# Renumbering the attention units so that the two halves of TensorE's array alternate (one-core streaming encoder step, f32)

## What is computed

```
B_HEAD_DIM = 64; B_Q_HEADS = 16; B_KV_HEADS = 4; CHUNK = 64; META = 16; WINDOW = 128
s_meta = jnp.einsum('bnqkgd,bjkd->bkgnqj', q, k_meta) * scale
s_loc = jnp.einsum('bnqkgd,bnjkd->bkgnqj', q, kb) * scale
p_meta, p_loc = sink_softmax(s_meta, s_loc, mask, sinks_r)
out = (jnp.einsum('bkgnqj,bjkd->bnqkgd', p_meta, v_meta)
       + jnp.einsum('bkgnqj,bnjkd->bnqkgd', p_loc, vb))
```

## Time and profile before

| | us |
|---|---|
| median of 3 runs (2803.07 to 2807.3) | 2803.46 |
| the profiled execution | 2798.76 |
| its span | 2797.0 |
| PE busy in the span | 2654.5 (95%) |
| attention block, its first DMA issue to the next block's first load | 1620.56 to 1817.31 |
| one prompt step of the loop | 7.66 |
| mean granted clock of TensorE over the span | 0.976 |

### The profile page before, as it was taken

One profiled execution on the slowest core, in us unless ns is written; L12 is line 12 of the kernel. 1 busy time (PEld: TensorE's weight loads), 2 busy tenths in 40 slices (PEclk: granted clock), 3 DMA queues, 4 the chain that ended last, 5 costly groups with the idle time before them and its releaser, 6 DMA issues. The chain is left out here.

```text
span 2797.0 us, 37740 instructions
## 1 busy us (share of the span) xinstructions
PE 2654.5 (95%) x15390; PEld 2593.3 (93%) x15390; DVE 1088.3 (39%) x2197; ACT 636.5 (23%) x1390; POOL 603.1 (22%) x503
## 2 busy tenths in 40 slices
PE   8999999989999999999978957898999999999998
PEld 7988898989999999999978946798999999999997
DVE  6444455153233333332374326524433333233334
ACT  5222223041111111111123314312211111111112
POOL 2212213211221222112233430022122212121211
PEclk9999999999999999999999969999999999999999
DMA  4544454111111111111113254331111111111111
GB/s 141 150 128 136 137 171 135 54 30 46 46 32 45 46 46 38 46 38 46 31 55 90 74 115 100 73 114 38 38 46 46 38 46 38 46 45 40 43 41 76
DMA packets 272768, 191.79 MB, mean 69 GB/s; under 512 B 53144, under 2 KB 259756, under 8 KB 272580
## 3 DMA queue, kind: packets, MB, share of 16 engines
q1 hardware_dynamic: 246324, 174.27, 21.4%
q10 hardware_dynamic: 25520, 15.04, 2.0%
q0 software_dynamic: 768, 0.27, 0.0%
HBM read 148.74 MB, written 42.34 MB: 68 GB/s over the span
## 5 line engine op out<-in xcount | busy, mean ns | idle before, releaser
L584 POOL TENSOR_TENSOR wl<-raw,wh 128x512 fp32r<-128x512 f32 x260 | 331.8, 1301 | 1329.5 <-ACT wh L576 1329.5
L706 PE MATMUL psum<-xh,wl 128*128 128x400 f32 (+1 forms) x1872 | 430.0, 338 | 0.0
L706 PE MATMUL psum<-xl,wh 128*128 128x400 f32 (+1 forms) x1872 | 428.3, 337 | 0.0
L706 PE MATMUL psum<-xh,wh 128*128 128x400 f32 (+1 forms) x1872 | 427.2, 336 | 0.0
L848 DVE TENSOR_TENSOR h<-h,psum 128x384 f32<-128x384 f32 (+1 forms) x528 | 264.5, 552 | 285.0 <-PE psum L726 267.3
L706 PEld LDWEIGHTS psum<-xh,wl 128*128 128x128 f32 x1872 | 336.6, 188 | 0.0
L706 PEld LDWEIGHTS psum<-xl,wh 128*128 128x128 f32 x1872 | 336.5, 188 | 0.0
L706 PEld LDWEIGHTS psum<-xh,wh 128*128 128x128 f32 x1872 | 335.8, 188 | 0.0
L1498 PE MATMUL psum<-xh,wh 128*128 128x384 f32 (+1 forms) x792 | 274.7, 347 | 5.2 <-DVE xl L1640 2.4
L1498 PE MATMUL psum<-xl,wh 128*128 128x384 f32 (+1 forms) x792 | 270.5, 342 | 0.0
L1498 PE MATMUL psum<-xh,wl 128*128 128x384 f32 (+1 forms) x792 | 269.4, 340 | 0.0
(11 more groups left out here) (237 smaller groups left out, 3582.1 us busy)
## 6 DMA issues: line engine op xcount, KB each, us to landing
raw<-in_w_gate_up SPq DMA_DIRECT2D x88, 512.0 KB, 3.9
raw<-in_w_down SPq DMA_DIRECT2D x44, 512.0 KB, 3.6
raw<-in_a_w_in SPq DMA_DIRECT2D x24, 512.0 KB, 4.7
fr_qkv<-qkv_d SPq DMA_DIRECT2D x36, 256.0 KB, 4.1
qkv_d<-fr_tmp SPq DMA_DIRECT2D x32, 192.0 KB, 2.0
qr_d<-tmp ACTq DMA_DIRECT2D x8, 584.0 KB, 2.8
x_loaded<-og_d SPq DMA_DIRECT2D x8, 584.0 KB, 5.7
hn_d<-fr_hn_turned SPq DMA_DIRECT2D x36, 128.0 KB, 3.3
```

The lines of the kernel that those rows point to most:

```text
L584: pool.tensor_tensor(wl[:, p % 3, v], raw[:, self.raw_of(p), v], wh[:, p % 3, v].bitcast(F32), ALU.subtract).then_inc(self.w_lo, 1)
L706: y = pe.matmul(psum[:, bank + c, 0:nt], w[:, k, :], x[:, k, t0:t0 + nt], start=(k == 0 and m == 0), stop=(k == KD - 1 and m == 2))
```

## The change

A table `UNITS` gives unit `un` its KV head and half: (0,0), (1,0), (0,1), (1,1), (2,0), (3,0), (2,1), (3,1). PE issues score and value matmuls in the order (kh 0, half 0), (kh 0, half 1), (kh 1, half 0), and so on, so neighbours use different halves of the array and, in the scores, different PSUM banks. In the values the two window matmuls of a pair come first, then the two meta matmuls. Decode scores loop over KV head, sequence, half, and each half has its own bank. The semaphores still count after four units. What follows from the numbering: the sinks are loaded by 8 smaller DMAs instead of 4, the waits for them go from 64 to 128, the decode maxima are two instructions instead of one, and the exponentials of decode look up where their unit's scores stand. The diff, cut:

```diff
+    UNITS = [(0, 0), (1, 0), (0, 1), (1, 1), (2, 0), (3, 0), (2, 1), (3, 1)]
+    PAIRS = [(kh, hf) for kh in range(KVH) for hf in range(2)]
...
-            pool.wait_ge(cst, 64)
+            pool.wait_ge(cst, 128)
...
-                    for b in range(SB):
-                        for un in range(NU):
-                            kh, half = un % KVH, HD * (un // KVH)
-                            x = pe.matmul(psum[R * b:R * b + R, 2 * g + un // 4, (un % 4) * SK:(un % 4 + 1) * SK],
+                    for kh in range(KVH):
+                        for b in range(SB):
+                            for hf in range(2):
+                                half = HD * hf
+                                x = pe.matmul(psum[R * b:R * b + R, 2 * g + hf, kh * SK:(kh + 1) * SK],
...
-                for un in range(NU):
-                    if later(i) and un % KVH == 0:
-                        pe.wait_ge(ex, i * 2 + (un // KVH - 1) if un else i * 2 - 1)
-                    kh, half = un % KVH, HD * (un // KVH)
+                for kh, hf in PAIRS:
+                    un, half = UNITS.index((kh, hf)), HD * hf
+                    if later(i) and hf == 0 and kh % 2 == 0:
+                        pe.wait_ge(ex, i * 2 if kh else i * 2 - 1)
...
-                    if kh == KVH - 1:
+                    if kh % 2 and hf:
                         x.then_inc(sc, 1)
...
-                for un in range(NU):
-                    kh, half = un % KVH, HD * (un // KVH)
-                    if kh == 0:
-                        pe.wait_ge(pts, i * 2 + (1 + un // KVH))
+                for kh in range(KVH):
+                    if kh % 2 == 0:
+                        pe.wait_ge(pts, i * 2 + (1 + kh // 2))
+                    outs = [psum[HD * hf:HD * hf + HD, 7, kh * P:(kh + 1) * P] for hf in range(2)]
+                    units = [UNITS.index((kh, hf)) for hf in range(2)]
                     if dec:
                         for b in range(SB):
-                            x = pe.matmul(psum[half:half + HD, 7, kh * P + R * b:kh * P + R * b + R],
-                                          vct[:, (i - NP) * SB + b, kh * HD:(kh + 1) * HD],
-                                          pt[0:SK, un, R * b:R * b + R], start=True, stop=True)
+                            for hf in range(2):
+                                x = pe.matmul(outs[hf][:, R * b:R * b + R],
+                                              vct[:, (i - NP) * SB + b, kh * HD:(kh + 1) * HD],
+                                              pt[0:SK, units[hf], R * b:R * b + R], start=True, stop=True)
                     else:
-                        o = psum[half:half + HD, 7, kh * P:(kh + 1) * P]
-                        pe.matmul(o, vw[0:w, kh * HD:(kh + 1) * HD], pt[0:w, un, :], start=True, stop=False)
-                        x = pe.matmul(o, vm[:, un, :], pm[:], start=False, stop=True)
+                        for hf in range(2):
+                            pe.matmul(outs[hf], vw[0:w, kh * HD:(kh + 1) * HD], pt[0:w, units[hf], :],
+                                      start=True, stop=False)
+                        for hf in range(2):
+                            x = pe.matmul(outs[hf], vm[:, units[hf], :], pm[:], start=False, stop=True)
...
-                        u = slice(KVH * half, KVH * half + KVH)
-                        act.dma_start(sink[j * CHUNK:(j + 1) * CHUNK, u], src.to_broadcast([CHUNK, KVH]))\
-                            .then_inc(cst, 16)
+                        for g in range(2):
+                            dst = sink[j * CHUNK:(j + 1) * CHUNK, 4 * g + 2 * half:4 * g + 2 * half + 2]
+                            act.dma_start(dst, src[:, 2 * g:2 * g + 2].to_broadcast([CHUNK, 2])).then_inc(cst, 16)
```

More of the change, by code:

```diff
@@ L2003, in _ @@
                 sp.dma_start(vm[META * un:META * un + META, un, :],
-                             kv[0:META, 0, 1, (un % KVH) * HD:(un % KVH + 1) * HD]).then_inc(vml, 16)
+                             kv[0:META, 0, 1, UNITS[un][0] * HD:(UNITS[un][0] + 1) * HD]).then_inc(vml, 16)
             load(2, WINDOW, 0)
@@ L2065, in scores @@
                         pe.wait_ge(ex, 2 * i)
-                    for b in range(SB):
-                        for un in range(NU):
-                            kh, half = un % KVH, HD * (un // KVH)
-                            x = pe.matmul(psum[R * b:R * b + R, 2 * g + un // 4, (un % 4) * SK:(un % 4 + 1) * SK],
-                                          qd[half:half + HD, g * SB + b, 2 * kh:2 * kh + 2, :],
-                                          ks[half:half + HD, g * SB + b, kh, :], start=True, stop=True)
+                    for kh in range(KVH):
[3 more added lines that the diff above has]
+                                x = pe.matmul(psum[R * b:R * b + R, 2 * g + hf, kh * SK:(kh + 1) * SK],
+                                              qd[half:half + HD, g * SB + b, 2 * kh:2 * kh + 2, :],
+                                              ks[half:half + HD, g * SB + b, kh, :], start=True, stop=True)
                     x.then_inc(sc, 2)
@@ L2179, in exponentials @@
                 for un in range(NU):
-                    x = act.activation(pb[:, u, un, 0:width(i)], src[:, un // per, un % per, :], ACT.Exp,
+                    at_ = UNITS[un][0] + KVH * UNITS[un][1] if decode(i) else un
+                    x = act.activation(pb[:, u, un, 0:width(i)], src[:, at_ // per, at_ % per, :], ACT.Exp,
                                        scale=SCORE_SCALE, bias=st[:, u, 2, un:un + 1], accum_out=st[:, u, 3, un:un + 1])
@@ L2216, in _ @@
                 dve.tensor_copy(kv[0:n, g, :, :].rearrange("p x d -> p (x d)"), psum[0:n, 4 + g, :]).then_inc(kve, 1)
-            dve.wait_ge(cst, 64)
+            dve.wait_ge(cst, 128)
             def maxima(i, u):
@@ L2224, in maxima @@
                 per = 4 if decode(i) else 2
-                out = st[:, u, 0, :].rearrange("p (b u) -> p b u", u=per)
-                halves = 1 if decode(i) else 2
-                m = NU // per // halves
-                for x in range(halves):
+                out = st[:, u, 0, :].rearrange("p (b u) -> p b u", u=2)
+                for x in range(2):
                     dve.wait_ge(sc, i * 2 + (2 if decode(i) else x + 1))
-                    y = dve.tensor_reduce(out[:, x * m:(x + 1) * m], unit_scores(i, per)[:, x * m:(x + 1) * m], AX_X,
-                                          ALU.max)
+                    if decode(i):
+                        out = st[:, u, 0, :].rearrange("p (g h k) -> p h g k", g=2, h=2)[:, x]
+                        src = unit_scores(i, per)[:, x].rearrange("p (g k) s -> p g k s", g=2)
+                        y = dve.tensor_reduce(out, src, AX_X, ALU.max)
+                    else:
+                        y = dve.tensor_reduce(out[:, 2 * x:2 * x + 2], unit_scores(i, per)[:, 2 * x:2 * x + 2], AX_X,
+                                              ALU.max)
                 y.then_inc(mx, 1)
```

## The result

The changed kernel takes 2776.01 us (median of 4 runs, 2775.57 to 2778.38) against 2803.69 of the kernel before in the same comparison: 27.7 us less, ratio 0.9903 with an interval of 0.989 to 0.9915. In the excerpts of traces and code, `...` stands for lines left out.

The account below looks back on a forecast made before the run. DVE and ACT were taken to bound the prompt loop, PE being late by only 0.24 us a step. Terms 3.4 + 3.2 + 1.5 + 3.2 + 1.5 - 0.2 = 12.6 us gave 2790.9 us; range 2781 to 2801.

Parts of the forecast that it names:

- (f): Sinks' 8 DMAs at the stage's start: nothing, ends +2.8 us or as much gained; split decode maxima cost 0.2 us.
- (a): Step 0's values and step 2's maxima at half clock: values 5.7 instead of 9.8 us, 3.4 us saved.
- (b): The 13 other prompt steps: DVE's remaining waits for prompt scores go, 3.2 us.
- (c): Step 3's values at half clock and the scores, after the cached keys are turned: 1.5 us gained, ends 0 and 2.7.
- The ceiling: Prompt loop: however fast PE becomes, a step can lose 0.24 us, not more.
- the ring: Prompt loop: dependencies through DVE and ACT set the step at about 7.42 us; it was 7.66 with PE late.
- (d): Two decode steps: prompt values ahead of each give 1.1 us, decode scores 0.5; together 3.2 us.
- the seam's rate: Where the old values switch halves, two units take 0.50 instead of 0.87 us; for decode scores 0.047 us per record.
- (e): Last 64 records of decode values, 6.61 us at half clock: 1.5 us gained, ends 0 and 2.8.
- rival "more": Whole attention: all ceilings reached and full clock back earlier, 22 us gained, 2781 us; chance 15%.
- rival of a loss by the clock: Prompt loop loses the full clock: +2.0 us a step, 2818 us with all twelve steps; chance 6%.
- signs that the prediction named for being wrong: Clock drops between 1700 and 1800 us, loop step stays at 7.66 us, or stage's first transposes move over 1 us.

Follow-up runs that it names:

- experiment 1: Kernel before with only the sinks loaded by 8 DMAs of two columns instead of 4 of four: 2797.64 us against 2805.35, ratio 0.998.
- experiments 2 and 6: Changed kernel with half the sinks' DMAs behind cached loads (2780.64 us), cached loads after K/V rows (2775.19), cached loads on SP (2776.29, 2771.6), sinks as one row (2775.6), last two together (2768.3).
- Experiment 4: Changed kernel with decode scores looping over sequence, KV head, half instead of KV head, sequence, half: one execution 2779.35 us.
- half of the sinks last: Changed kernel with four of its eight sink DMAs issued behind the loads of cached keys and decode queries: 2780.64 us, ratio 0.9914.
- cached keys on SP: Changed kernel with cached keys, values and decode queries loaded on SP's queue behind step 2's loads, GpSimd's weight preparation split: 2776.29 us, ratio 0.9903.
- step 3 ahead: Changed kernel with cached loads on SP, step 3's Q, K and V loads issued ahead of them, GpSimd's first weights prepared later: 2771.6 us, ratio 0.9889.
- both: Changed kernel with cached loads on SP behind step 3's loads, and sinks loaded as one row to each partition: 2768.27 us, ratio 0.9877.

## Why the prediction was wrong

**(f) failed, and is the largest error: 0 forecast, 6.35 us measured at the first maxima.** The step read: "so I take nothing", as the cached keys are needed late and DVE comes late to its wait for the sinks. Both are true and beside the point: the question was what else is in the queues. What experiment 1 shows in its place is that the eight DMAs alone bring the first maxima 6.4 us forward and the time to 0.998 of the old one, some 6 us less. That they do it because ACT's later cached loads let SP's K and V rows go first is read from the queues; experiments 2 and 6 give the position of the cached loads and the pieces of the sinks a part each.

**(a) came to its number partly by luck, and was eaten: 3.4 forecast, 3.66 measured, then 2.62 us lost** in step 2 to 3, where the earlier statistics of DVE met GpSimd's split. I had asked what comes late on PE's path, not what a neighbour does at the new time. The 3.4 us were what a wait for K ahead of step 2's scores would leave, and that wait did not come (the one of 3.78 us came in step 1, where it cost nothing: maxima 0 to 1 are 5.69 us apart before and 5.70 after). PE's rows from step 0's values to its next transposes:

```profile
1650.65 0.69 PE L2121 MATMUL psum<-at_prob_turned,at_v_window 64*64 64x128 f32 x4 [1.92 <-DMA at_v_meta<-at_kv_rows]
1651.27 0.69 PE L2124 MATMUL psum<-at_prob_meta_turned,at_v_meta 128*64 128x128 f32 x4
...
1655.63 0.69 PE L2061 MATMUL psum<-ident,at_v 128*128 128x128 f32 x2
```

A group of two takes 0.62 us, what one matmul took before (0.61), not 0.71; the values take 4.98 instead of 9.83 us. What held the gain down was another transfer, the meta rows of V: the values start 4.95 us after the second maxima instead of 2.82.

**(b) and (c): 4.7 forecast, 5.0 measured.** The ceiling held as a mechanism, but the ring was 7.33 and not 7.42 us: when PE is early, the maxima follow the V copy after 0.33 instead of 0.42 us. A pair costs 0.44 us, not the 0.50 of the one seam in the old order, whose neighbours on either side still ran alone.

**(d): 3.0 forecast, 5.5 measured.** The failed step was "I take 0.5, being next to the seam's rate". That the old order overlaps here already was right, but the seam's rate (0.047 us per record, scaled from another form) is that of two tiles at work and no floor. Experiment 4 shows 1.95 us with two tiles in strict turn and 1.00 with eight, 0.016 us per record (1.00 / 64); even the end of half of 3.29 us was passed.

**(e): 1.5 forecast, 4.9 measured.** The failed step was to take the middle between nothing and 2.8 us: the values overlap fully, at either clock (6.61 to 3.63, 3.68 to 2.06), so the order alone gives 3.0. The other part is the clock, which stayed up in the profiled execution. The rival "more" named both, with 2.8 us for this term and 15% for the case, and was still 5 us short, since a gain by (f) was in no case.

The rival of a loss by the clock, at 6%, came in a small dose. The stretch of 1700 to 1740 us, before and after:

```profile
1700.00:1740.00 40.00, 34.73 (x311) 30.80 (x309) 26.79 (x65) 19.13 (x91) 0.00 (x0) 1.00 0.53 115
```

```profile
1700.00:1740.00 40.00, 26.91 (x312) 22.58 (x313) 29.27 (x73) 19.66 (x99) 0.00 (x0) 0.94 0.60 130
1726.00:1728.00 2.00, 2.00 (x20) 1.62 (x16) 1.05 (x4) 0.91 (x6) 0.00 (x0) 0.50 0.00 0
```

With PE less busy the clock is at its lower level for parts of the loop. The changed kernel's loop steps are 7.32 to 7.35 us but for one of 7.42, so it paid 0.1 us; in four of the other kernels with the new order (half of the sinks last, cached keys on SP, step 3 ahead, both) one step of the loop took 8.35 us. Of the signs that the prediction named for being wrong, two were there: this drop of the clock, and the first transposes of the stage, which moved from 23.21 to 16.85 us after its start.

With three of the changed kernel's terms off by 6.4, 2.5 and 3.4 us in the same direction, a range of 10 us on either side could not hold the time. It was built from the bounds of the terms, and the one bound that was passed over was that of (f), whose working named a gain of 2.8 us as an end; in the range it stood on the slow side only.

What stays open: 5 of the 27.7 us stand between the medians and the profiles, since the profiled execution of the kernel before was 4.7 us faster than its median. The last values don't explain it, since that execution had them at the lower clock already. The first decode values can be slow too (5.74 instead of 3.68 us in the profile of experiment 1), which would be 2 of the 4.7. And the step from 4 to 5, with the cached keys' turns, varies from 15.9 to 17.3 us between kernels with the same instructions of PE and DVE there; no run tells why.

## What to carry to other kernels

Matmuls that use a part of the array overlap only as far as neighbours in program order go to different tiles: list the tile of each matmul in that order and count how many differ in a row, and don't take the best rate seen so far for a floor when the form has more tiles. Price each added or moved DMA by what is queued on all queues behind it, above all with pieces of a few bytes, and not by who needs its data. When an engine becomes early, look up what its neighbour does at the new time: here DVE met GpSimd and gave back 2.6 us of 3.7. And a PE that works faster between the same waits is idle more: the clock of its loop fell from 1.00 to 0.94.

## What the runs showed of the hardware

- Decode scores of the 64*32 form took 3.36, 1.95 and 1.00 us for the same 64 records, with the tile changing after every four matmuls, with two tiles in turn, and with eight. Records of one tile start 0.083 us apart.
- While GpSimd runs an operation with two inputs of 1024 columns, a DVE operation on 8 columns of SBUF, 0.17 us by itself, took 1.26, 1.82 and 2.31 us; maxima read from PSUM took their usual 0.76. The Trainium skill, GPSIMD Engine Reference, 1. Specifications, says that its SBUF interface is shared with VectorE; the trace agrees, and it shows the price: in all three cases DVE's operation ended when GpSimd's did.
- The same loads of new V rows landed after 12.1, 8.2 and 2.4 us, with the sinks in pieces and the cached keys close behind them, with the cached keys 2.6 us later, and with neither in front.
- With the same program the last decode values ran at either level of the clock: 6.61 and 3.68 us.
